# First modulation vectors by column pairs, and the first two projection chunks between them

## The reference, cut to what matters

```
mod_x = (silu_c @ w_mod[l] + b_mod[l])[:, None, :]
sh1, sc1, gt1, sh2, sc2, gt2 = jnp.split(mod_x, 6, axis=-1)
mod_c = (silu_cc @ w_mod[l] + b_mod[l])[None, None, :]
hc = modulate(rms_norm(ctx, g_norm1[l]), csh1, csc1)
hx = modulate(rms_norm(x, g_norm1[l]), sh1, sc1)      # modulate: x * (1 + scale) + shift
proj = h @ p['w_in']                                  # (tokens, 1024) @ (1024, 2304)
```

## Time and profile before

| | us |
|---|---|
| median of 3 runs (1560.53 to 1562.51) | 1561.42 |
| span of the profiled execution | 1559.4 |
| PE, busy share of the span | 95% |
| first matmul of a `w_in` chunk in the trace | 40.13 |
| first matmul of the third `w_in` chunk | 64.94 |

### The profile page before, as it was taken

One profiled execution on the slowest core, in us unless ns is written; L12 is line 12 of the kernel. 1 busy time (PEld: TensorE's weight loads), 2 busy tenths in 40 slices (PEclk: granted clock), 3 DMA queues, 4 the chain that ended last, 5 costly groups with the idle time before them and its releaser, 6 DMA issues.

```text
span 1559.4 us, 21947 instructions
## 1 busy us (share of the span) xinstructions
PE 1477.2 (95%) x8714; PEld 1041.6 (67%) x8715; DVE 838.9 (54%) x1135; ACT 617.5 (40%) x698; POOL 17.4 (1%) x56
## 2 busy tenths in 40 slices
PE   5999798999999999897879999999999999999997
PEld 3786486788888887783755566565766566565754
DVE  2899945333333333799564554445554555545552
ACT  3425723322122222439344333434443444434442
POOL 2000000000000000100010000000000000000000
PEclk8999899999999999999889999999999999999998
DMA  9633933921542233348159999989999999999992
GB/s 360 199 100 106 363 108 129 236 75 56 146 116 78 69 93 125 102 142 331 49 217 395 340 330 337 343 323 407 381 408 405 403 385 401 408 379 404 383 409 105
DMA packets 208006, 395.44 MB, mean 254 GB/s; under 512 B 12044, under 2 KB 123040, under 8 KB 207904
## 3 DMA queue, kind: packets, MB, share of 16 engines
q1 hardware_dynamic: 207312, 393.80, 70.2%
q10 hardware_dynamic: 592, 0.21, 0.1%
HBM read 392.93 MB, written 1.05 MB: 253 GB/s over the span
## 4 chain that ended last, share of the span: by engine, by line
PE 87%; DVE 4%; ACT 4%; DMA 2%; issue 2%; DVEq 0%; ACTq 0%
PE bank L757 85%; PE bank L1248 1%; DMA raw<-in_w_mod 1%; DMA raw<-in_moe_w 1%; DVE tb L1828 1%; ACT la L1532 1%; DVE y L1957 0%; DVE h_lo L1836 0%; ACT lr L1526 0%; PE bank L1193 0%; DMA rows_sb<-in_b_mod 0%; ACT lm L1574 0%; PE bank L782 0%; ACT li L1528 0%; ACT lm L1539 0%
## 5 line engine op out<-in xcount | busy, mean ns | idle before, releaser
L2265 DVE TENSOR_TENSOR w_lo<-raw,w_hi 128x2048 fp32r<-128x2048 f32 x132 | 302.4, 2292 | 260.5 <-ACT w_hi L1653 260.5
L1653 ACT ACTIVATE w_hi<-raw 128x2048 fp32r<-128x2048 f32 x132 | 252.4, 1912 | 402.1 <-PE bank L757 285.5
L757 PE MATMUL bank<-h_hi,w_hi 128*128 128x512 f32 (+1 forms) x768 | 285.2, 371 | 13.1 <-DVE h_lo L1836 12.0
L757 PE MATMUL bank<-h_lo,w_hi 128*128 128x512 f32 (+1 forms) x768 | 283.0, 368 | 0.0
L757 PE MATMUL bank<-h_hi,w_lo 128*128 128x512 f32 (+1 forms) x768 | 282.9, 368 | 0.0
L1411 ACT ACTIVATE w_hi<-raw 128x2048 fp32r<-128x2048 f32 (+1 forms) x64 | 113.7, 1776 | 209.8 <-PE bank L757 196.0
L757 PEld LDWEIGHTS bank<-h_hi,w_hi 128*128 128x128 f32 x768 | 147.2, 192 | 38.8 <-DVE h_lo L1836 13.4
L757 PEld LDWEIGHTS bank<-h_lo,w_hi 128*128 128x128 f32 x768 | 147.2, 192 | 23.5
L757 PEld LDWEIGHTS bank<-h_hi,w_lo 128*128 128x128 f32 x768 | 146.9, 191 | 23.5
L1811 DVE TENSOR_TENSOR w_lo<-raw,w_hi 128x2048 fp32r<-128x2048 f32 (+1 forms) x64 | 136.0, 2124 | 36.8 <-ACT w_hi L1411 36.6
L757 PE MATMUL bank<-w_hi,hc_hi 128*128 128x512 f32 (+1 forms) x384 | 153.1, 399 | 2.4 <-ACT warm L1708 2.4
(11 more groups left out here) (307 smaller groups left out, 1796.6 us busy)
## 6 DMA issues: line engine op xcount, KB each, us to landing
raw<-in_moe_w SPq DMA_DIRECT2D x220, 1024.0 KB, 9.0
raw<-in_w_mod SPq DMA_DIRECT2D x48, 1024.0 KB, 8.7
raw_x<-in_moe_w SPq DMA_DIRECT2D x44, 1024.0 KB, 8.9
raw<-in_ffn_w SPq DMA_DIRECT2D x44, 512.0 KB, 5.3
raw<-in_w_in SPq DMA_DIRECT2D x18, 1024.0 KB, 5.4
raw<-in_ffn_w SPq DMA_DIRECT2D x16, 704.0 KB, 4.5
raw<-in_w_out SPq DMA_DIRECT2D x8, 1024.0 KB, 5.7
x_in<-in_ctx SPq DMA_DIRECT2D x1, 1024.0 KB, 5.0
```

Source lines behind the costliest of these rows:

```text
L757: return nc.tensor.matmul(dst, lhsT, rhs, start=first, stop=last)
L1653: nc.scalar.activation(w_hi[:, j % SPL, :], raw[:, E_SLOT[j], :], ACT.Copy)\
L2265: V.tensor_tensor(w_lo[:, j % SPL, :], raw[:, E_SLOT[j], :], w_hi[:, j % SPL, :].bitcast(F32), ALU.subtract).then_inc(dve_done, dve_n(name ...
```

## The change

- The load order becomes: tokens, modulation quarter 0 of shift and of scale, `w_in` chunks 0 and 1, the quarters 1 to 3 of shift and scale, and then the third `w_in` chunk. A quarter is all 1024 rows of 256 columns of its vector, so each line of such a load is 1 KB long where it was 4 KB.
- One quarter pair gives shift and scale for two blocks of channels. PE works it with as many matmuls as two old chunks (`quarter_rows`), ACT copies both rows in one instruction (`quarter_row`), four small matmuls turn them into columns (`quarter_columns`), and DVE finishes them (`quarter_modulated`).
- The mean squares come from the tokens' rows: ACT squares `x_in` with a sum along the row (four instructions of 128x1024), takes the root of four columns, DVE inverts them, and four matmuls spread them (`tok_ms`). The eight squares of `xT` and PE's sums of them go away in this stage.
- The first two `w_in` chunks are multiplied block by block, with the next quarter's matmuls behind the even blocks and its columns in the middle of the odd ones (`started`). The blocks 6 and 7 come at the end, first half, tables, second half.
- The splits `low(0)` and `low(1)` stay with the first blocks; `hi(2)` and `low(2)` move behind the last block.

```diff
-    chunks = [("mod", l, q, kq) for l, q in START_MODS for kq in range(MOD_K)] + SPLIT[:SPL]
+    chunks = []
+    for c4 in range(QUARTERS):
+        chunks += [("quarter", q, c4) for _, q in START_MODS]
+        if c4 == 0:
+            chunks += SPLIT[:EARLY]
+    chunks += SPLIT[EARLY:SPL]
...
+            def started():
+
+                pe.wait_ge(act_done, at("cc"))
+                quarter_rows(0)
+                pe.wait_ge(dve_done, at("r", 0, 1))
+                for n in range(4):
+                    i = mm(STAT[:, P * n:P * n + P], tok_ms[:, 4 + n:5 + n].to_broadcast([P, P]), ident[:, :], True, True)
+                i.then_inc(pe_done, pe_n("rs", 0, 1))
+                quarter_columns(0)
+                for k in range(KD):
+                    pe.wait_ge(dve_done, at("h_lo", 0, 1, k))
+                    if k == 0:
+                        take(("w_in", 0, WIN_ORDER[0]))
+                    if k < KD - 2:
+                        for t in range(2):
+                            product(0, 0, t, k)
+                        if k % 2:
+                            quarter_columns(k // 2 + 1)
+                        if k == 0:
+                            take(("w_in", 0, WIN_ORDER[1]))
+                        for t in range(2):
+                            product(0, 1, t, k)
+                        if k % 2 == 0:
+                            quarter_rows(k // 2 + 1)
+                for t in range(2):
+                    for n in range(EARLY):
+                        for k in range(KD - 2, KD):
+                            product(0, n, t, k)
+                    if t == 0:
...
+                        for m in range(1, len(TABLES)):
+                            i = tables(m)
+                        i.then_inc(pe_done, pe_n("tables"))
...
+                    for c4 in range(QUARTERS):
+                        quarter_row(c4)
+                        if c4 == 0:
+                            hi(0)
+                        for d in (2 * c4, 2 * c4 + 1):
+                            start_high(d)
+                        if c4 == 0:
+                            hi(1)
+                    hi(2)
...
+                if (l, w) == (0, 1):
+                    for c4 in range(QUARTERS):
+                        quarter_modulated(c4)
+                        for d in (2 * c4, 2 * c4 + 1):
+                            t_of(d)
+                        if c4 == 0:
+                            low(0)
+                        for d in (2 * c4, 2 * c4 + 1):
+                            lo_of(d)
+                        if c4 == 0:
+                            low(1)
+                    low(2)
+                    return
```

More of the change, by code:

```diff
@@ L440, in weights @@
             l = c[1]
+            if c[0] == "quarter":
+                w = a["w_mod"][0].rearrange("(k p) c -> p k c", p=P)
+                return w[:, :, D * c[1] + 256 * c[2]:D * c[1] + 256 * c[2] + 256]
             if c[0] == "mod":
@@ L543, in _ @@
                              a[name][0].rearrange("(t p) c -> p t c", p=P)).then_inc(tokens_in[s], 16)
[L544 to L547, removed]
+            for c in CHUNKS:
                 if c == GATES_BEFORE:
@@ L881, in first_products @@
[L881 to L890, removed]
+                    product(l, 1, 0, k)
@@ new lines, in first_products, with quarter_rows @@
+                    product(l, 0, 1, k)
+                    product(l, 1, 1, k)
+            def quarter_rows(c4):
+                pe.wait_ge(dve_done, at("xT", "in", 4 + c4 % 2))
+                for _, q in START_MODS:
+                    c = ("quarter", q, c4)
+                    slot = POS[c] % RAW
+                    pe.wait_ge(raw_in[slot], arrived[c])
+                    for kk in range(2):
+                        for g in range(GROUPS):
+                            o = 256 * (2 * g + kk)
+                            i = mm(bank[4 + c4 % 2][MOD_W * g:MOD_W * g + MOD_W, 256 * q:256 * q + 256],
+                                   cc[:, 2 * g + kk, :], raw[:, slot, o:o + 256], kk == 0, kk == 1)
+                    i.then_inc(pe_done, pe_n("used", *c))
@@ L918, in _ @@
                 if l == 0:
[L919 to L929, removed]
+                    started()
                 else:
@@ L1465, in _ @@
                 ts = slice(lo[l], T)
-                squares(l, 1, slice(0, T), ("in",) if l == 0 else ("down", 1), range(KD) if l == 0 else [KD - 1])
-                root(l, 1, slice(0, T))
                 if l == 0:
-                    hi(0)
-                h_high(l, 1, (0, 1), h_hi, "h_hi")
+                    for s in range(2):
+                        act.wait_ge(tokens_in[s], 16)
+                        for t in range(2):
+                            n = 2 * s + t
+                            nc.scalar.activation((la, lm)[s][:, 2 * t:2 * t + 2, :].rearrange("p k c -> p (k c)"),
+                                                 x_in[:, s, D * t:D * t + D], ACT.Square, accum_out=tok_ms[:, n:n + 1])\
+                                .then_inc(act_done, act_n(*(("tok_sq",) if n == 3 else ())))
@@ new lines, in start_high @@
+                    def start_high(d):
+                        act.wait_ge(dve_done, at("t", 0, 1, d))
+                        for s in range(2):
+                            i = nc.scalar.activation(h_hi[:, d, tok(s)], tb[:, d % 2, tok(s)], ACT.Identity,
+                                                     bias=modT[:, 0, d, s:s + 1])
+                            i.then_inc(act_done, act_n(*(("h_hi", 0, 1, d) if s else ())))
+                    for c4 in range(QUARTERS):
[6 more added lines that the diff above has]
+                            hi(1)
@@ L1471, in _ @@
+                    hi(2)
+                else:
+                    squares(l, 1, slice(0, T), ("down", 1), [KD - 1])
+                    root(l, 1, slice(0, T))
+                    h_high(l, 1, (0, 1), h_hi, "h_hi")
                 s0, s1 = ORD[("w_in", l, 0)], ORD[("w_in", l, 1)]
```

77 lines of the change are left out of this document (50 added, 27 removed).

## The result

The changed kernel takes 1566.53 us (median; 1565.63 to 1569.70), the kernel before beside it 1561.58 us (1560.53 to 1563.37). The ratio is 1.0034, with a 95% interval from 1.0023 to 1.0045: slower by 4.9 us by the medians (5.3 by the ratio, 3.6 to 7.0 by its interval). A second set of executions gave 1.0030 (1.0019 to 1.0041). The forecast was 1566.7, slower.

The account below looks back on a forecast made before the run. Loads were taken to bound the start until the first product at 40.13, PE itself the stage after it. +1.85 us at full clock and +3.4 for two clock falls gave +5.25, median 1566.7 us, range 1561.0 to 1570.0.

Parts of the forecast that it names:

- Loads: Start of the kernel: quarters with 1-KB lines load at 350 GB/s, 3.0 us each, first pair there at 16.0.
- Squares: Start, on ACT: four row squares of 1.05 us and a root end at about 16, hidden behind the first pair.
- First product: End of the start-up chain: PE's first product at 24.7, 15.4 us earlier than 40.13.
- The pace of the blocks: First two chunks: 3.4 us from columns to product, PE idles of 2.0, 2.0 and 2.9, 10.6 between even blocks.
- The falls: Behind PE's three idles in the first stage: two drops to half clock, +3.4 us together.
- the rise of the first fall: Behind the first products: full clock returns between 30.3 and 33.3, quarter pair 1 taken to end at 33.3.
- I cost this at nothing: Behind the tables: DVE 2.8 us later against PE, taken up by waits of 2.78 near 143 and 148.
- VectorE's lag: Tables and taps: VectorE 2.8 us later against PE because `low(2)` stands behind the last block.
- the holding clock: Rival, first stage: the clock stays up through the three idles, only +1.85, 1563.3 us; chance 0.22.
- The hidden hand-over: Rival, block loop: VectorE and ScalarE prepare the next pair while PE works, -5.9, 1555.5 us; chance 0.07.
- the unabsorbed lag: Rival, taps and gate stage: VectorE's 2.8 us delay comes on top of the forecast, 1569.5 us; chance 0.11.

Follow-up runs that it names:

- rowsq: Kernel before with one part of the change alone, the mean squares from the tokens' rows; 1562.34 us, ratio 1.0006.
- slow: Changed kernel with one small hand-over step (a pair's amplitude on VectorE) done six times instead of once, in all four pairs; 1571.91 us, ratio 1.0070.
- early: Changed kernel with rows and columns of quarter pairs 2 and 3 both put inside the even block ahead; 1562.66 us, ratio 1.0015.
- lag: Changed kernel with the third `w_in` chunk's halves split behind pair 2 instead of pair 3; 1565.85 us, ratio 1.0037.
- after_again: Changed kernel measured once more with no edit; 1566.35 us, ratio 1.0030.
- pad: Changed kernel with 20 empty instructions at TensorE's start, where it waits for the first load; 1565.89 us, ratio 1.0037.
- lastwarm: Changed kernel with eight spare TensorE matmuls meant for the late idle, placed by mistake at 1014.7 us; 1575.58 us, ratio 1.0084.
- fill: Changed kernel with 14, 14 and 20 spare matmuls in TensorE's idles of blocks 1, 3 and 5; 1563.48 us, ratio 1.0008.
- best: Changed kernel, pairs wholly inside even blocks, spare matmuls in the first idle and those of blocks 1 and 5, eight misplaced ones; 1562.62 us, ratio 1.0006.

## Why the prediction was right

Total and sign came out as forecast (+5.25, measured +4.9), but not quite along its path: the stage's delay was too large by 2.6 us, and some 2.3 us that it did not have came in elsewhere. That the two nearly cancel is luck; the first product, the hand-over and the waits are not.

- **Loads.** Forecast 3.0 us for a quarter at 350 GB/s. The windows of 10:12 and 20:22 show 349 and 348, 12:14 shows 318. In after PE took the second half of pair 0 without a wait, as its transposes lasted to 15.0 and not 13.9. Right, and the Trainium skill's 512 B as the smallest transfer at line rate ("DMA: Bandwidth & Descriptors", Specifications) is again not what the rows show: 1-KB lines 349, 4-KB lines 401.
- **Squares.** Forecast four of 1.05, done at 16, hidden. They took 1.04 each with 0.19 for a readout that mostly ran beside the next; the root came at 15.69. Right, and rowsq shows them as free.
- **First product.** Forecast 24.7, measured 24.33: `rs` 1.16, columns 0.95 (forecast 1.0), the hand-over to `tb` 0.6 (0.55), `tb` 1.66, `low(0)` 2.28 (2.2).
- **The pace of the blocks.** Forecast 3.4 from the end of the columns to the product and idles of 2.0, 2.0 and 2.9; measured 3.3 and 1.78, 1.79 and 2.69. From block to block 12.1 (36.54 to 48.66) against 10.6 and a fall; without the fall 10.5. The cause is shown twice, by slow (+0.98 in every pair) and by early (-1.4 for six matmuls).
- **The falls.** Two forecast at 1.7 each, two came in the profile, at 1.6 by lag. "Not each one will do it" was the right reading: the same idle of 1.8 brings a fall in after and none in early. The number is not the kernel's own: after, after_again and pad have two falls, but lastwarm, whose first stage is that of after, has one (0.63 in 38:40, 0.52 in 40:42), and so has lag.
- **The step that failed** is the rise of the first fall: "I put the rise between 30.3 and 33.3", and so pair 1 ends at 33.3. The clock was back at 27.4, matmuls at 0.23 us apart from 27.69 on, and the pair's rows ended at 30.8. Block 2 started at 36.54 instead of 39.05; 0.4 of this had come with the first product. So the third chunk starts at 67.57 instead of 70.2, and the delay at the end of the run is 2.64 instead of 5.25. The forecast took its 5.5 us from first product to rise from before, where it was 5.7 (45.8) after an idle of 5.39. There the clock had fallen long before that idle (0.86 in 28:29, 0.50 from 29 on); here it fell inside an idle of 5.31, and the rise took 3.1. Nor is this one number for the changed order: by their windows it took 3.0 in after_again, 3.8 in lastwarm, 4.6 in lag and 5.3 in early, after the same idle. Lastwarm's run ends at 142.77, so its stage is 1.5 us late where that of after is 2.64. The length of a rise isn't to be carried from one place to another, nor from one execution to the next.
- **Downstream.** "I cost this at nothing" holds for VectorE's lag: PE is 2.64 late at 143.9 and still 2.64 late at 185.74 (183.10 before). Only the reason for the lag was off: `low(2)` ended at 63.2, ahead of the tables' transposes, which stand late in PE's order. It doesn't hold for the rest. In the profile the gap at 1371 costs 1.8 us and that at 1546 0.4 more than before's. The end behind VectorE's last instruction is 1.0 longer; this is no chance, as it is 4.7 us in nine of the ten profiles of the changed order (3.8 in slow) and 3.7 in the four of the old one, but 0.4 of it comes back outside the span (2.1 us before, 1.7 after). With the 2.64 this makes 5.4 us, beside 4.9 by the medians and 5.3 by the ratio. The causes of these three stay open, and so does how often each comes: single profiles can't tell it.

Of the rivals, the holding clock is out for this kernel (two falls seen in the profile, and fill recovers their price), though fill itself comes out where the rival would have: 1.0008. By the Trainium skill ("TensorE: Matmul & The Clock Gate", HAM oscillation) long bursts should hold the clock; the rows show busy stretches of 9 to 10 us with idles of 1.8 that let it fall at 37.6 and hold it at 48.7. The hidden hand-over is out by the idles themselves, and the unabsorbed lag by the unchanged 2.64 behind it.

## What to carry to other kernels

A transfer taken out of the start is worth only what the chain behind it doesn't take back: count the hand-over from engine to engine (here 3.3 us, from PE over VectorE, ScalarE and VectorE back to PE) and set it against the work that the bound engine has between producing and needing, 1.36 here; put twice as much between and most of the wait is gone. Price idles of a bound TensorE with the clock they may cost, as a range and not as a number, and fill them with spare matmuls to find out. And when a change of code moves a time far from its place, look at the gaps without a releaser at a loop's jump back and behind the loops before looking for a cause in the data.

## What the hardware showed that I had not expected

- Equal idles, unequal clocks: 1.78 us was followed by a fall (36.54) and 1.79 was not (48.66), in one execution; the late idle was followed by 3 to 4 us at 0.5 to 0.7 in five kernels (2.50 to 2.56 long) and by no fall in eight executions of others (2.26 to 2.64).
- After idles of the same length (5.3 us) the clock rose 3.0 to 5.3 us after the first product in profiles of the changed order (3.1 in after, 5.3 in early), and 5.7 us after it in before.
- Eight matmuls of PE (16 passes) placed at 1014 us go with a gap of 8.19 us at 1367 in the changed kernel, and with none in before and in best.
- An activation with a sum along the row is two instructions in the trace: 1.04 us for 128x1024 and 0.19 for the readout.
